# The mixers of a hybrid decoder step: another order, and the skip term as products with diagonal matrices

## What is computed

```python
y_diag = einsum('bcijgr,bcjgrp->bcigrp', cb[..., None] * decay * dtc[:, :, None], xc)
y_off  = einsum('bcign,bcigr,bcgrpn->bcigrp', cc, exp(cum), h_prev)
y = (y_diag + y_off).reshape(b, s, nh, hp)
y = y + xs * d_skip[:, None]                 # the skip term
y = y.reshape(b, t, D_SSM) * silu(z)         # the gate
yg = y.reshape(b, t, SSM_GROUPS, D_SSM // SSM_GROUPS)
yg = yg * rsqrt(mean(yg * yg) + EPS)
```

## Time and profile before

| | |
|---|---|
| median of 3 runs | 1880.09 us |
| profiled execution | 1877.65 us, span 1875.8 us |
| mean granted clock of TensorE | 0.992 |
| busy: TensorE, VectorE, GpSimd, ScalarE | 1798.2, 1406.7, 1083.5, 916.0 us |

### The profile page before, as it was taken

How to read it: one execution, slowest core, us unless ns; L and a number is a source line. 1 busy time by engine, 2 the same in 40 slices (tenths; PEclk the granted TensorE clock), 3 DMA queues, 4 the chain that set the end, 5 groups by cost and what they waited for, 6 DMA issues and landing times.

```text
span 1875.8 us, 33881 instructions
## 1 busy us (share of the span) xinstructions
PE 1798.2 (96%) x12872; PEld 1668.2 (89%) x12872; DVE 1406.7 (75%) x1933; ACT 916.0 (49%) x1694; POOL 1083.5 (58%) x876
## 2 busy tenths in 40 slices
PE   8999999999999999989979999899999999999999
PEld 7999999888888899855557899899999999999999
DVE  5788850699888777589987555897777779778776
ACT  5344422577777788578851023343333344444442
POOL 4588740577767666346552124355555568787774
PEclk9999999999999999989999999999999999999999
DMA  4444442745554443599975543224334376443432
GB/s 177 147 149 189 171 158 65 156 123 116 132 131 105 128 134 102 192 366 348 357 229 209 182 149 130 88 86 190 127 146 154 143 267 240 144 158 130 149 138 94
DMA packets 139100, 309.34 MB, mean 165 GB/s; under 512 B 31659, under 2 KB 65323, under 8 KB 135228
## 3 DMA queue, kind: packets, MB, share of 16 engines
q1 hardware_dynamic: 115356, 271.15, 43.4%
q10 hardware_dynamic: 23584, 36.04, 5.7%
HBM read 222.42 MB, written 93.28 MB: 168 GB/s over the span
## 4 chain that ended last, share of the span: by engine, by line
PE 73%; DVE 10%; issue 5%; DMA 5%; ACT 4%; POOL 2%; SPq 1%; ACTq 0%; DVEq 0%; POOLq 0%
PE ff_ps L2727 31%; PE proj_ps L469 9%; PE dense_ps L1055 7%; PE wo_psa L2565 5%; PE proj_ps L552 3%; PE att_t_ps L1087 2%; PE wo_psb L2694 2%; DVE silu_half L1216 2%; PE wo_psa L2694 1%; PE att_s_ps L1073 1%; PE att_s_ps L1074 1%; DVE att_p L1169 1%; PE att_pv_ps L1104 1%; PE att_pv_ps L1102 1%; DMA sa_v<-in_cache_v 1%
## 5 line engine op out<-in xcount | busy, mean ns | idle before, releaser
L2727 PE MATMUL ff_ps<-ff_set,ff_wring 128*128 128x264 f32 x5376 | 661.4, 286 | 9.0 <-DVE ff_set L3337 3.2
L2727 PEld LDWEIGHTS ff_ps<-ff_set,ff_wring 128*128 128x128 f32 x5376 | 659.0, 189 | 11.0 <-DVE ff_set L3337 3.6
L2399 POOL TENSOR_TENSOR ff_wring<-const,ff_wring 128x256 fp32r<-128x256 f32 (+1 forms) x192 | 213.7, 1117 | 146.6 <-ACT ff_wring L2892 146.0
L985 POOL TENSOR_SCALAR att_p<-att_p,att_rden 128x128 f32<-128x128 f32 (+6 forms) x112 | 196.9, 1767 | 117.3 <-DVE att_rden L1147 116.9
L2892 ACT ACTIVATE ff_wring<-const 128x256 fp32r<-128x256 f32 (+1 forms) x192 | 93.6, 489 | 221.8 <-PE ff_ps L2727 112.8
L3359 DVE TENSOR_TENSOR h<-h,ff_ps 128x528 f32<-128x528 f32 x192 | 133.1, 700 | 49.6 <-PE ff_ps L2727 46.1
L1282 ACT ACTIVATE att_pThi<-att_t_ps 128x512 fp32r<-128x512 f32 x192 | 93.3, 487 | 93.3 <-PE att_t_ps L1087 79.7
L1055 PE MATMUL dense_ps<-u_hi,w_hi 128*128 128x352 f32 x480 | 121.9, 335 | 4.7 <-POOL w_lo L254 2.2
L1169 DVE CUSTOM_DVE_ANT_0 att_p<-att_s_ps,att_bias 128x128 f32<-128x128 f32 (+7 forms) x128 | 94.8, 753 | 38.1 <-PE att_s_ps L1074 34.9
L1055 PE MATMUL dense_ps<-u_hi,w_lo 128*128 128x352 f32 x480 | 119.4, 330 | 0.0
L1156 DVE TENSOR_TENSOR att_pTlo<-att_t_ps,att_pThi 128x512 fp32r<-128x512 f32 x192 | 104.3, 550 | 20.0 <-ACT att_pThi L1282 19.4
(11 more groups left out here) (384 smaller groups left out, 4332.7 us busy)
## 6 DMA issues: line engine op xcount, KB each, us to landing
tmp_r_sets<-h SPq DMA_DIRECT2D x16, 1848.0 KB, 6.3
ff_setraw<-tmp_r_sets SPq DMA_DIRECT2D x56, 528.0 KB, 5.4
sa_k<-in_cache_k SPq DMA_DIRECT2D x32, 640.0 KB, 6.3
sa_v<-in_cache_v SPq DMA_DIRECT2D x40, 512.0 KB, 6.3
w_raw<-in_w_feat SPq DMA_DIRECT2D x36, 512.0 KB, 6.3
out_qk<-proj_out SPq DMA_DIRECT2D x16, 528.0 KB, 8.0
tmp_bias_rows<-tmp_table ACTq DMA_DIRECT2D x8, 1024.0 KB
att_bias<-tmp_bias_rows SPq DMA_DIRECT2D x16, 512.0 KB, 3.5
```

Of the source, the lines that this page charges most:

```text
L985: pool.tensor_scalar(slot(h, qt), slot(h, qt), rden[:, qt, :], None, ALU.mult).then_inc(normed, 1)
L2399: pool.tensor_tensor(w_set(n)[:, 1], operand(q, m), w_set(n)[:, 0].bitcast(F32), ALU.subtract).then_inc(fw_split, 1)
L2727: mm = pe.matmul(ff_ps[:, (b + g) * 512:(b + g) * 512 + HG], ws[:, wi, k, :], xs[:, xi, k, g * HG:(g + 1) * HG], start=(opens and k == 0 a ...
```

## The change

The skip term is no longer added by VectorE. GpSimd makes eight diagonal 128x128 matrices of the skip weights once, `skip_diag`, and each tile in `inner` begins with a matmul of its diagonal by x, which opens the bank; the others accumulate. `add_skip` and its semaphore go. `gate(n, g)` multiplies the bank by z straight out of PSUM, a group at a time, in iteration n itself, where add_skip stood. `load_z(n+1)` is issued in iteration n, ahead of load_v(n+1). The rows load is cut into two halves, one in front of load_k. `turn_x(n+1, 0)` moves from behind value 1 to before value 0, and `turn_x(n+1, 1)` to behind value 1; `weigh(n+1, 0)` moves ahead of `split_v(n, 3)`, and ScalarE does casts and segments in another order. Iteration 0 keeps its old order for most of this. Semaphores, `load_rows` at the start and the outward stage are adapted. The core of the diff:

```diff
@@ -1579,23 +1580,24 @@
                 if n >= 2:
                     sp.wait_ge(x_turned, 2 * (n - 1))
                     sp.wait_ge(bcb_made, n - 1)
-                    sp.wait_ge(y_skipped, 2 * (n - 1))
+                    sp.wait_ge(gated, 2 * (n - 1))
                 if n >= 3:
                     sp.wait_ge(grown_made, 2 * (n - 2))
                 sp.dma_start(xbc[j][:], dram["xbc"][:, cols].rearrange("(f p) t -> p f t", p=P)).then_inc(loaded[j], 16)
 
             def load_z(n):
                 if n:
-                    sp.wait_ge(gated, n)
+                    sp.wait_ge(gated, 2 * n)
                 sp.dma_start(zT[:], dram["z"][:, n * P:(n + 1) * P].rearrange("(f p) t -> p f t", p=P)
                              ).then_inc(z_loaded, 16)
 
-            def load_rows(n):
+            def load_rows(n, g):
+                hs = slice(8 * g, 8 * g + 8)
                 if n >= 2:
-                    sp.wait_ge(in_made, 2 * (n - 1))
-                sp.dma_start(mixm[n % 2][:].rearrange("p h t -> p (h t)"),
-                             dram["cum_rows"][n * NH:(n + 1) * NH, :].rearrange("h t -> (h t)").partition_broadcast(P)
-                             ).then_inc(rows_loaded[n % 2], 16)
+                    sp.wait_ge(in_made, 2 * (n - 2) + g + 1)
+                sp.dma_start(mixm[n % 2][:, hs, :].rearrange("p h t -> p (h t)"),
+                             dram["cum_rows"][n * NH + 8 * g:n * NH + 8 * g + 8, :].rearrange("h t -> (h t)").partition_broadcast(P)
+                             ).then_inc(rows_loaded[2 * (n % 2) + g], 16)
 
             def load_k(b):
                 for u in range(KB):
...
@@ -1641,14 +1645,15 @@
             for j in range(2):
                 sp.wait_ge(woven.mix_stored[j], 16 * NPAIR)
             for n in range(NC):
+                if n + 2 < NC:
+                    load_rows(n + 2, 0)
                 if n + 1 < NC:
                     load_k(n + 1)
-                if n:
-                    load_z(n)
                 if n + 2 < NC:
                     load_chunk(n + 2)
-                    load_rows(n + 2)
+                    load_rows(n + 2, 1)
                 if n + 1 < NC:
+                    load_z(n + 1)
                     load_v(n + 1)
                 if n == NC - 2:
                     ahead.load(sp, dram)
@@ -1757,8 +1762,10 @@
             def inner(n, g):
                 if g == 0:
                     pe.wait_ge(x_kept, 2 * n + 2)
+                if n == 0:
+                    pe.wait_ge(zeroed, 6)
                 if n:
-                    pe.wait_ge(y_skipped, 2 * n + g - 1)
+                    pe.wait_ge(gated, 2 * n + g - 1)
                     pe.wait_ge(grown_made, 2 * n + g - 1)
                     pe.wait_ge(state_summed, 2 * n + g - 1)
                 for f in range(4):
...
-                        mm = pe.matmul(out(r), xdt[:, cols(r)], mixm[n % 2][:, 8 * g + 2 * f + r, :], start=True, stop=(n == 0))
+                        mm = pe.matmul(out(r), xdt[:, cols(r)], mixm[n % 2][:, 8 * g + 2 * f + r, :], start=False, stop=(n == 0))
                     if n:
                         for r in range(2):
                             mm = pe.matmul(out(r), state[:, cols(r)], grown[g][:, 2 * f + r, :], start=False, stop=True)
@@ -1815,6 +1824,8 @@
                         chunk_start(n + 1)
                     sample_turn(n)
                     states(n, 1)
+                    if n + 1 < NC:
+                        turn_x(n + 1, 0)
                 else:
                     states(n, 0)
                     inner(n, 0)
@@ -1825,17 +1836,17 @@
                     chunk_start(n + 1)
                 sample_values(n, 1)
                 if n + 1 < NC:
-                    turn_x(n + 1, 0)
+                    turn_x(n + 1, 1 if n else 0)
                 sample_values(n, 2)
                 if n == 0:
-                    pe.wait_ge(zeroed, 5)
+                    pe.wait_ge(zeroed, 6)
                     pe.wait_ge(v_cast, VS + 1)
                     pe.wait_ge(v_split, VS + 1)
                 sample_new_values(n)
-                if n + 1 < NC:
-                    turn_x(n + 1, 1)
                 if n:
                     norm_sums(n - 1)
+                else:
+                    turn_x(1, 1)
                 sample_values(n, 3)
                 sample_values(n, 4)
             mixed.pe_tail = sample_gather, turn_out, norm_sums
...
@@ -1903,12 +1914,14 @@
             pool.wait_ge(woven.ring.made, woven.dense)
             pool.memset(p_new[3 * NS:P, :].bitcast(F32), 0.0).then_inc(zeroed, 1)
             pool.wait_ge(zeroed, 4)
+            pool.tensor_tensor(skip_diag[:], kit.c(C_IDENT, P).unsqueeze(1).broadcast_to([P, KD, P]),
+                               skip[:].unsqueeze(2).broadcast_to([P, KD, P]), ALU.mult).then_inc(zeroed, 1)
             weigh_x(0)
             pool.wait_ge(woven.tail_stored, 16)
             pool.wait_ge(woven.feat_stored, woven.stores)
             pool.wait_ge(xw_made, 1)
             pool.memset(new_stack[3 * NS:P, :].bitcast(F32), 0.0).then_inc(zeroed, 1)
-            pool.wait_ge(zeroed, 5)
+            pool.wait_ge(zeroed, 6)
             for n in range(NC):
                 if n:
                     decay(n, 0)
...
@@ -1931,8 +1945,8 @@
         def _(act):
             def segment(n, q):
                 m = mixm[n % 2]
-                if q == 0:
-                    act.wait_ge(rows_loaded[n % 2], 16 * (n // 2 + 1))
+                if q % 2 == 0:
+                    act.wait_ge(rows_loaded[2 * (n % 2) + q // 2], 16 * (n // 2 + 1))
                 for h in range(4 * q, 4 * q + 4):
                     act.activation(m[:, h, :], m[:, h, :], ACT.Relu, bias=cum[:, n, h:h + 1],
                                    scale=-1.0).then_inc(seg_low, 1)
@@ -1941,7 +1955,7 @@
                                scale=-1.0).then_inc(seg_exp, 1)
 
             def grow_exp(n, g):
-                act.wait_ge(rows_loaded[n % 2], 16 * (n // 2 + 1))
+                act.wait_ge(rows_loaded[2 * (n % 2) + g], 16 * (n // 2 + 1))
                 if n >= 2:
                     act.wait_ge(in_made, 2 * n + g - 1)
                 act.activation(grown[g][:], mixm[n % 2][:, 8 * g:8 * g + 8, :], ACT.Exp).then_inc(grown_exp, 1)
@@ -1985,10 +1999,9 @@
                                accum_out=den[:]).then_inc(exped, 1)
 
             def square(n):
-                act.wait_ge(gated, n + 1)
+                act.wait_ge(gated, 2 * n + 2)
                 if n:
                     act.wait_ge(normed, n)
-                act.wait_ge(y_skipped, 2 * n + 2)
                 act.activation(sq[:], y_all[:, :, n * P:(n + 1) * P], ACT.Square).then_inc(squared, 1)
 
             segment(0, 0)
@@ -2003,16 +2016,24 @@
                 act.wait_ge(woven.mix_stored[j], 16 * NPAIR)
             keep_probs(0)
             for n in range(NC):
-                for t in range(VS):
-                    cast_v(n, t)
-                if n == 0:
+                cast_v(n, 0)
+                if n:
+                    if n + 1 < NC:
+                        grow_exp(n + 1, 0)
+                        segment_next(n + 1, 0)
+                    cast_v(n, 1)
+                    cast_v(n, 2)
+                    if n + 1 < NC:
+                        segment_next(n + 1, 1)
+                else:
+                    cast_v(0, 1)
+                    cast_v(0, 2)
                     act.wait_ge(new_loaded, 48)
                     act.wait_ge(woven.feat_stored, woven.stores)
                     act.activation(new_stack[0:3 * NS, :], own[0:3 * NS, :], ACT.Copy).then_inc(v_cast, 1)
-                if n + 1 < NC:
-                    grow_exp(n + 1, 0)
-                    segment_next(n + 1, 0)
-                    segment_next(n + 1, 1)
+                    grow_exp(1, 0)
+                    segment_next(1, 0)
+                    segment_next(1, 1)
                 if n:
                     exponent(n)
                     square(n - 1)
@@ -2041,19 +2062,11 @@
                 dve.tensor_tensor(cb, cb, kit.c(C_UPPER, P).unsqueeze(1).broadcast_to([P, 2, P]),
                                   ALU.mult).then_inc(cb_masked, 1)
 
-            def add_skip(n, g):
+            def gate(n, g):
                 dve.wait_ge(in_made, 2 * n + g + 1)
-                for f in range(4 * g, 4 * g + 4):
-                    op = dve.scalar_tensor_tensor(out=y_all[:, f, n * P:(n + 1) * P], in0=xbc[n % 2][:, f, :],
-                                                  scalar=skip[:, f:f + 1], in1=y_ps[g][:, f % 4 * P:(f % 4 + 1) * P],
-                                                  op0=ALU.mult, op1=ALU.add)
-                op.then_inc(y_skipped, 1)
-
-            def gate(n):
-                dve.wait_ge(y_skipped, 2 * n + 2)
-                yt = y_all[:, :, n * P:(n + 1) * P]
                 dve.wait_ge(z_loaded, 16 * (n + 1))
-                dve.tensor_tensor(yt, yt, zT[:], ALU.mult).then_inc(gated, 1)
```

(21 more changed lines are left out.)

## The result

The kernel after took 1899.45 us (median of 4 runs, 1893.6 to 1899.67), the kernel before 1879.24 in the same comparison: 1.0102 times as long, interval 1.0087 to 1.0118. The forecast was 1886.5, between 1879.5 and 1893. The sign was right, the size was not. The profiled execution took 1899.38 us, with a span of 1897.5.

A forecast was written before the change was run, and what follows sets the result against it. TensorE was busy 96% of the span, with VectorE and DMA close in a steady chunk. Start +1.5, five chunks +5.0, chunk 7 +1.2 and end -1.2 made +6.5 us: median 1886.5, range 1879.5 to 1893.

The forecast's parts named there:

- The price of a diagonal: TensorE in `inner`: each added skip matmul costs 0.225 us, eight add 1.8 us a chunk, bounds 1.45 and 2.15.
- chunk 7: Last chunk of the mixers stage: the added 1.8 us less 0.61 us of TensorE idling before sample_turn, +1.2 us.
- The order's gain: TensorE in a steady chunk: turning x earlier removes stalls, gaining 0.8 us and not 2.1.
- left-over stalls: TensorE ahead of values 3 and 4: waits of 0.4 and 0.8 us remain in a steady chunk.
- Rival C: GpSimd's weigh_x takes the lock ahead of split_v(n, 4): +2.9 us a chunk, about 1898 us; chance 0.10.
- Rival A: Stalls ahead of values 3 and 4 do close: chunk stays 21.4 to 21.5 us, total 1881.6; chance 0.25.
- B: Faster: matmul costs 0.18, `split_v` not held, chunk 1's data wait shrinks; about 1875.4 us; chance 0.13.
- VectorE's relief counted at nothing: Steady chunk: 2.5 us off VectorE gains nothing, since no steady TensorE stall ends with `add_skip` or `gate`.
- The start: Chunks 0 and 1: split_new and TensorE's new values move later, +1.5 us, between 0 and +3.5.
- covered: Chunks 0 and 1: the added matmuls lie before the waits for data and so cost nothing.
- wait of the first gate for z: VectorE in chunk 0: the gate must wait for z(0), landing about 809.7; split_new moves by 1.3 to 2 us.
- The last gate: End of the kernel: the 1.22 us gate disappears from between two `split_a`, -1.2 us, between 0 and -2.

## Why the prediction was right or wrong, step by step

**The price of a diagonal was the miss.** 0.225 us with bounds of 0.18 and 0.27, and 0.505 measured: 8 x 0.28 = 2.2 us a chunk. Over five chunks that is 11.2 us, against the 10.7 by which these came out too long, and over chunk 7 another 2.2 of 2.7. All three rows that I had were of a matmul among its like: a pair between pairs, the full-height products of `chunk_start` and those of `norm_sums` among themselves. None was a full-height one between halves, and from them I took the one that was "nearest". With like neighbours the number is right: 0.22 in halves, 0.25 in one block. What the sum lacked was a line for the change of height: seven of them in a group, where there had been one. The rule of the Trainium skill above speaks against this change, and I had not weighed it. The trace of before had the one change, in TensorE's timeline from value 4 into `inner`:

```profile
842.19 0.63 PE L1699 MATMUL sa_s<-sa_vlo,sa_pT 128*64 128x512 f32 x2
842.66 0.63 PE L1695 MATMUL sa_s<-sa_vhi,sa_pT 128*128 128x512 f32 x2
843.22 0.44 PE L1775 MATMUL ssd_in<-ssd_m,ssd_xdt 128*64 128x128 f32 x4
843.49 0.39 PE L1778 MATMUL ssd_in<-ssd_grown,ssd_state 128*64 128x128 f32 x4
843.71 0.39 PE L1775 MATMUL ssd_in<-ssd_m,ssd_xdt 128*64 128x128 f32 x4
```

The full-height row takes 0.56 us to the next one, the half-height row ahead of it 0.47 with as many columns, and the first pair 0.27 where the second takes 0.22. So 0.14 us stood there for one change from full to half. Six changes more in each group at that price would have added 2 x 6 x 0.14 = 1.7 us a chunk to the sum, of the 2.2 that were measured. It took a row at the border of `inner` to see it: the changes of height between values 0 and 1, in the same trace, show no such price.

**The order's gain was right.** 0.8 us a chunk forecast, 0.72 measured in the changed kernel, 0.6 by taking it out again (25.23 - 24.61) and 0.5 by itself (21.46 - 20.96). The left-over stalls, 0.4 and 0.8 forecast, are 0.40 and 0.57. The same lock makes them. VectorE's and GpSimd's timelines of the kernel after:

```profile
864.72 2.28 DVE L2122 TENSOR_TENSOR sa_vlo<-sa_v,sa_vhi 128x1024 fp32r<-128x1024 f32 x1 [0.81 <-ACT sa_vhi L1990]
...
867.53 1.21 DVE L2122 TENSOR_TENSOR sa_vlo<-sa_v,sa_vhi 128x1024 fp32r<-128x1024 f32 x1
```

```profile
863.52 2.41 POOL L1892 TENSOR_TENSOR ssd_grown<-ssd_grown,ssd_xbc 128x1024 f32<-128x1024 f32 x1
...
867.69 2.82 POOL L1880 TENSOR_TENSOR ssd_xw<-ssd_xdt,ssd_decays 128x1024 f32<-128x1024 f32 x1 [1.76 <-DVE ssd_xdt L2076]
```

`split_v(n, 3)` at 864.72 ends 1.07 us after `grow` (865.93), as in the earlier trace rows.

**Rival C** gave nearly the right total, 1898, by the wrong mechanism. At its point VectorE was first, at 867.53, and it is GpSimd's `weigh_x` that is held, for 2.82 us and not 1.91. A total alone would have taken it for shown. **Rival A** falls by the same stalls, and **B** by every chunk.

**VectorE's relief counted at nothing:** right for the changed kernel, since no wait of TensorE in its steady chunk ends with either operation. It was also smaller than its sum of 2.5 us: VectorE's busy time in a chunk fell by 1.4, from 19.86 to 18.44. Its other side, that ScalarE's new order depends on it, was not seen.

**The start,** +1.5 forecast and +1.9 measured: the size is near, but the way there is not shown. The diagonals are dearer still at its beginning. TensorE's timelines of inner(0, 0), before and after:

```profile
801.63 1.98 PE L1775 MATMUL ssd_in<-ssd_m,ssd_xdt 128*64 128x128 f32 x16
803.53 1.48 PE L1754 MATMUL ssd_off<-ssd_xw,ssd_btok 128*128 128x512 f32 x2
```

```profile
801.72 0.77 PE L1781 MATMUL ssd_in<-ssd_xbc,ssd_skipdiag 128*128 128x128 f32 x2 [0.17 <-issue]
...
807.10 2.08 PE L1759 MATMUL ssd_off<-ssd_xw,ssd_btok 128*128 128x512 f32 x2
```

The group takes 5.38 us where it took 1.90, with a granted clock of 0.50 over the group in both, which is the 1.2 GHz level: (5.38 - 1.90) / 4 = 0.87 for each diagonal. A window over that stretch of the kernel after has TensorE busy for 18.77 of 19.30 us, against 15.53 before:

```profile
801.70:821.00 19.30, 18.77 (x90) 11.55 (x92) 13.41 (x18) 12.68 (x27) 3.85 (x4) 0.75 1.03 334
```

Still, "covered" held. The run without the skip term takes 43.4 us from inner(0, 0) to inner(2, 0), and the changed kernel 43.5. TensorE is busy for 36.39 of these us at a granted clock of 0.80 in the one, and for 41.79 at 0.89 in the other: the diagonals fill what the other run spends idle and at the lower clock. The forecast's wait of the first gate for z does exist, and is seen where no diagonals hide it. VectorE's timeline of the run without the skip term:

```profile
810.83 0.69 DVE L2066 TENSOR_TENSOR h<-ssd_in,ssd_z 128x512 f32<-128x512 f32 x1 [2.41 <-DMA ssd_z<-tmp_z]
```

But the run of all the orders on the kernel before has neither this gate nor the earlier load of z, and its start is the longest of all, 43.8 us. Between 42.3 and 43.8 us were seen for this stretch in the eight kernels with ScalarE's new order, and between 41.0 and 42.7 in the six with the old one. With one profile each, what makes the start longer stays open.

**The last gate,** -1.2 forecast and nothing measured (+0.1 from the first value of chunk 7 on). In the earlier trace rows it stands between two `split_a`. TensorE's timeline of before has a wait right behind it:

```profile
980.31 0.91 PE L2565 MATMUL wo_psa<-mix_split,wo_hi 128*128 128x352 f32 x4 [1.36 <-DVE mix_split L3026]
```

In the kernel after, that wait is gone, but others have grown: those of 0.3 us or more for `split_a` up to the last one add up to 4.6 us (0.85, 0.53, 2.09, 1.14), where they were 5.0 (1.36, 0.79, 0.45, 0.33, 2.08). Against this, the first products of `outward` took 3.10 us at a granted clock of 0.62 (996.65 to 999.75), where before they took 2.03 at 1.00 (975.04 to 977.07). So by this trace 0.4 of the 1.2 us came, and the lower clock took back more than that. Why it was lower there was not tried.

## What to carry to other kernels

Price a matmul by a row with the same neighbours, not by one with the same shape. Here every way from small half-height pairs to a full-height product and back cost 0.34 us extra, though the values change their height at no such price; look for a row at such a border. Cutting the tall product in halves saves all of it, gathering the tall ones in a block most of it. Before work is moved to TensorE, leave it out altogether and look at the chunk: here even a free skip term gave nothing over the old place on VectorE. And where two engines exclude each other, the cheap cure may be to hold the one that nobody waits for.

## What the runs showed that was not expected

- A 128x128 fp32 product of 128 columns takes 0.25 us among its like, 0.22 as two halves among halves, and 0.505 alone between halves; the price goes with the number of blocks, 2.78, 3.12, 3.47, 3.82 us.
- In a group with a granted clock of 0.50 the same product between halves cost 0.87 us.
- The values change between 128 and 64 output rows too, and their loads start 0.22 to 0.23 us ahead as if nothing changed.
- Two matmuls in place of each diagonal made the kernel 14.7 us faster than one.
- Whether GpSimd's `grow` starts 0.76 us ahead of VectorE's `split_v` or together with it decides between chunks of 22.0 and 20.0 us, in one and the same execution.
